# A two-layer attention step on one core: cached keys and values loaded in blocks of 128 rows

## The reference, cut to what matters

```python
s = jnp.concatenate([
    jnp.einsum('bqhcd,bkhcd->bhcqk', q, k_past), jnp.einsum('bqhcd,bkhcd->bhcqk', q, k_new)], axis=-1) * scale
p = jax.nn.softmax(s, axis=-1)
pd = p[:, :, 0] - lam * p[:, :, 1]
o = jnp.einsum('bhqk,bkhe->bqhe', pd[..., :p_len], v_past) + jnp.einsum('bhqk,bkhe->bqhe', pd[..., p_len:], v_new)
```

```python
s_past = einsum('bqhd,bkhd->bhqk', q, k_past) * scale + f_q[..., None] - f_bht[:, :, None, :p_len]
```

## Time and profile before

| what | us |
|---|---|
| median of 3 runs | 2518.02 (2517.57 to 2519.05) |
| the profiled execution, own time | 2516.69 |
| its span, first to last instruction | 2514.2 |
| stage A, about | 629 to 765 of the span |
| stage B, about | 1865 to 2015 of the span |

### The profile page before, as it was taken

The page is one execution under the profiler, slowest core; times in us unless marked ns, Lnnn a source line. Parts: engine busy times, 40 slices in busy tenths (PEclk is TensorE's granted clock), DMA queues, the critical chain, the costliest instruction groups (busy, mean ns, idle before and its releaser), DMA issues.

```text
span 2514.2 us, 46820 instructions
## 1 busy us (share of the span) xinstructions
PE 2463.0 (98%) x18869; PEld 2333.4 (93%) x18869; DVE 1687.4 (67%) x2936; ACT 1134.2 (45%) x2261; POOL 192.3 (8%) x136
## 2 busy tenths in 40 slices
PE   8999999999898999999999999999998899999998
PEld 8999999888678999999988999999986599999998
DVE  7777676322797886758625786858626677868585
ACT  6443444101785543435413553525327755535254
POOL 0000000543000000000044000000120000000000
PEclk9999999999999999999999999999999999999999
DMA  4323232233762232323233332222359631322222
GB/s 129 91 72 95 70 99 61 82 117 102 293 236 76 63 105 62 99 76 91 62 80 125 106 109 81 74 87 72 114 192 314 226 109 47 111 79 74 86 72 80
DMA packets 267136, 271.45 MB, mean 108 GB/s; under 512 B 13785, under 2 KB 224034, under 8 KB 266930
## 3 DMA queue, kind: packets, MB, share of 16 engines
q1 hardware_dynamic: 261184, 253.45, 32.4%
q10 hardware_dynamic: 5746, 15.12, 1.7%
HBM read 255.02 MB, written 13.51 MB: 107 GB/s over the span
## 4 chain that ended last, share of the span: by engine, by line
PE 90%; DVE 5%; ACT 2%; issue 2%; DMA 1%; DVEq 0%; POOL 0%; ACTq 0%
PE PS L769 40%; PE PS L875 24%; PE PS L956 10%; PE PS L719 7%; PE PS L707 2%; PE PS L1014 1%; PE PS L702 1%; PE PS L1157 1%; PE PS L1115 1%; DMA R<-in_cache_b_k_dram 1%; PE PS L1076 1%; PE PS L1087 1%; DVE x_area L2050 0%; DVE R L2005 0%; ACT R L1646 0%
## 5 line engine op out<-in xcount | busy, mean ns | idle before, releaser
L769 PE MATMUL PS<-x_area,w_area 128*128 128x320 f32 x3096 | 482.1, 309 | 0.0
L769 PEld LDWEIGHTS PS<-x_area,w_area 128*128 128x128 f32 x3096 | 461.0, 188 | 0.2 <-DVE w_area L1991 0.2
L875 PE MATMUL PS<-r_area,w_area 128*128 128x320 f32 x2568 | 393.3, 309 | 0.0
L875 PEld LDWEIGHTS PS<-r_area,w_area 128*128 128x128 f32 x2568 | 380.7, 188 | 0.8 <-DVE r_area L2183 0.8
L1435 ACT ACTIVATE w_area<-R 128x512 fp32r<-128x512 f32 x341 | 212.7, 628 | 200.4 <-PE PS L769 133.0
L1982 DVE TENSOR_TENSOR w_area<-R,w_area 128x768 fp32r<-128x768 f32 (+2 forms) x143 | 132.4, 926 | 218.5 <-ACT w_area L1420 216.9
L1991 DVE TENSOR_TENSOR w_area<-R,w_area 128x512 fp32r<-128x512 f32 x341 | 234.4, 688 | 47.6 <-ACT w_area L1435 41.8
L1420 ACT ACTIVATE w_area<-R 128x768 fp32r<-128x768 f32 (+2 forms) x143 | 117.0, 818 | 308.2 <-PE PS L875 281.2
L875 PE MATMUL PS<-v_area,w_area 128*128 128x320 f32 x1620 | 253.5, 309 | 0.0
L956 PE MATMUL PS<-w_area,xn_hi 128*128 128x512 f32 x800 | 251.0, 395 | 0.0
L875 PEld LDWEIGHTS PS<-v_area,w_area 128*128 128x128 f32 x1620 | 241.5, 188 | 0.3 <-DVE v_area L2183 0.3
(11 more groups left out here) (297 smaller groups left out, 3566.6 us busy)
## 6 DMA issues: line engine op xcount, KB each, us to landing
R<-in_w_ffn_up_dram SPq DMA_DIRECT2D x88, 512.0 KB, 3.9
R<-in_w_ffn_gate_dram SPq DMA_DIRECT2D x84, 512.0 KB, 3.9
R<-in_w_ffn_down_dram SPq DMA_DIRECT2D x96, 384.0 KB, 3.2
vreg<-in_cache_a_v_dram SPq DMA_DIRECT2D x8, 2048.0 KB, 9.0
vreg<-in_cache_b_v_dram SPq DMA_DIRECT2D x8, 2048.0 KB, 9.5
R<-in_cache_a_k_dram SPq DMA_DIRECT2D x14, 1024.0 KB, 7.2
R<-in_cache_b_k_dram SPq DMA_DIRECT2D x14, 1024.0 KB, 9.8
R<-in_w_qkv_a_dram SPq DMA_DIRECT2D x24, 512.0 KB, 3.8
```

The source lines that it names most:

```text
L769: last = pe.matmul(PS[:, bank, 0:HT], a[:, k, :], b[:, k, :], start=(start and k == 0 and a is hi and b is x_hi), stop=(k == 3 and a is lo ...
L875: last = pe.matmul(out[:, h, :], a[slot][:, w], x[:, h * HT:(h + 1) * HT], start=(k == 0 and a is w_hi and x is hi), stop=(k == n - 1 and ...
```

## The change

The loads change from 1 MB of keys and 2 MB of values to blocks of 128 rows, 512 KB each in pieces of 4 KB, for keys and values alike. `Knat` becomes four row blocks. `key_turn(b, j)` turns block j of all eight heads, as many turns and copies of the same size as `key_pair` had. Each step now waits for its own block, and block k of the next but one stream can be asked for as soon as block k has been turned. Keys use two semaphores (even and odd blocks) and values two, and before asking for block k SP waits until block k-2 of the same tensor has landed. The first keys of a stage are loaded in two halves by rows, and each of the eight `first_keys` waits for both halves.

In B the keys of stream 1 stay ahead of the values; two of their blocks now stand between the forget rows. The diff, cut to its core (PE, ACT and DVE call `key_turn` at the places where they called `key_pair`, and that is left out):

```diff
 nat = R1[:, 0:2 * TB * D].rearrange("p (w t c) -> p w t c", w=2, t=TB)
-Knat = R1[:, 0:4096].rearrange("p (s k c) -> p s k c", s=2, k=PB)
+Knat = R1[:, 0:4096].rearrange("p (k c) -> p k c", k=PB)
 kTc = R1[:, 4096:8192].rearrange("p (h k) -> p h k", h=PAIR)
...
 
-def load_keys(queue, x, b, s):
-    queue.dma_start(Knat[:, s], key_rows[x][b, :, s * 512:(s + 1) * 512].rearrange("(k p) c -> p k c", p=P)).then_inc(
+def load_first_keys(queue, x, s):
+    queue.dma_start(Knat[:, 2 * s:2 * s + 2, :], key_rows[x][0, 256 * s:256 * s + 256, :].rearrange("(k p) c -> p k c", p=P)).then_inc(
         sem(f"k_in{x}{s}"), 16)
+
+def keys_landed(b, k):
+
+    return 16 + (b - 1) * 32 + (k // 2 + 1) * 16
+
+def values_landed(x, b, k):
+
+    return ("AB".index(x) * DB + b) * 32 + (k // 2 + 1) * 16
...
 
-        def keys(b, s):
-            load_keys(sp, x, b, s)
-
-        def values(b):
-            sp.dma_start(Vc, vc[b].rearrange("(k p) c -> p k c", p=P)).then_inc(sem("v_in" + x), 16)
+        def keys(b, k):
+            at = sem(f"k_in{x}{k % 2}")
+            sp.wait_ge(at, keys_landed(b, k) - 16)
+            sp.dma_start(Knat[:, k, :], key_rows[x][b, k * P:(k + 1) * P, :]).then_inc(at, 16)
+
+        def values(b, blocks):
+            for k in blocks:
+                at = sem(f"v_in{k % 2}")
+                if k >= 2:
+                    sp.wait_ge(at, values_landed(x, b, k) - 16)
+                sp.dma_start(Vc[:, k, :], vc[b][k * P:(k + 1) * P, :]).then_inc(at, 16)
...
 
-        sp.wait_ge(sem("kt_ready" + x), 4)
-        keys(1, 0)
         if x == "A":
+            sp.wait_ge(w_used, BASE["oa"])
+            values(0, range(PB))
+            sp.wait_ge(sem("kt_readyA"), 8)
+            for k in range(PB):
+                keys(1, k)
             tile(BASE["oa"], SLOT["oa"], *cols(w_o_a[0], SLOT["oa"], 0))
-            sp.wait_ge(sem("kt_readyA"), 8)
+        else:
+            sp.wait_ge(sem("kt_readyB"), 8)
+            keys(1, 0)
             keys(1, 1)
-            sp.wait_ge(w_used, BASE["oa"])
-        else:
             sp.wait_ge(w_used, BASE["ob"] - 1)
             rows(0)
             forget(0, 0)
+            keys(1, 2)
+            keys(1, 3)
             sp.wait_ge(sem("sq_used"), 4 * KB)
             forget(0, 1)
             rows(1)
-            sp.wait_ge(sem("kt_readyB"), 8)
-            keys(1, 1)
             sp.wait_ge(w_used, BASE["ob"])
-        values(0)
+            values(0, range(PB))
         for i in range(DB - 1):
+            more = i + 2 < DB
             if f_scr is not None:
                 sp.wait_ge(sem("biased" + x), i * 2 + 2)
                 forget(i + 1, 0)
                 forget(i + 1, 1)
-            if i + 2 < DB:
-                sp.wait_ge(sem("kt_ready" + x), (i + 1) * 8 + 4)
-                keys(i + 2, 0)
-            if f_scr is not None and i + 2 < PAIR:
-                sp.wait_ge(sem("nb_ready" + x), i * 4 + 4)
-                rows(i + 2)
+            for k in range(3):
+                if more:
+                    sp.wait_ge(sem("kt_ready" + x), (i + 1) * 8 + 2 * k + 2)
+                    keys(i + 2, k)
+                if k == 1 and f_scr is not None and i + 2 < PAIR:
+                    sp.wait_ge(sem("nb_ready" + x), i * 4 + 4)
+                    rows(i + 2)
             sp.wait_ge(sem("pv_ready" + x), i * 2 + 2)
-            values(i + 1)
-            if i + 2 < DB:
+            values(i + 1, (0, 1))
+            if more:
                 sp.wait_ge(sem("kt_ready" + x), (i + 1) * 8 + 8)
-                keys(i + 2, 1)
+                keys(i + 2, 3)
+            values(i + 1, (2, 3))
 
     for c in range(4):
...
 
-        pe.wait_ge(sem(f"k_in{x}{h // 4}"), 16)
+        for s in range(2):
+            pe.wait_ge(sem(f"k_in{x}{s}"), 16)
         if h >= 2:
             pe.wait_ge(sem("first_read" + x), h - 1)
         for k in range(PB):
-            last = flip(PS[:, bank, k * P:(k + 1) * P], Knat[:, h // 4, k, (h % 4) * P:(h % 4 + 1) * P])
+            last = flip(PS[:, bank, k * P:(k + 1) * P], Knat[:, k, h * P:(h + 1) * P])
         last.then_inc(sem("kt_ready" + x), 1)
...
+        reads, first_reads = (5, 2) if x == "A" else (4, 1)
+
+        def key_turn(b, j):
 
             if b == DB:
                 return
-            if j % 2 == 0:
-                pe.wait_ge(sem(f"k_in{x}{j // 2}"), b * 16 + 16)
+            pe.wait_ge(sem(f"k_in{x}{j % 2}"), keys_landed(b, j))
             if j == 0:
                 pe.wait_ge(sem("sexp_doneA" if x == "A" else "biasedB"), b * 2)
                 if x == "B" and b >= 2:
                 if x == "A" and b >= 3:
                     pe.wait_ge(sem("columns_readA"), b - 2)
             else:
-                pe.wait_ge(sem("pairs_read" + x), (b - 1) * reads + first_pair_reads + j - 1)
-            for h in range(2):
-                at = (2 * j + h) % 4 * P
-                for k in range(PB):
-                    for r in range(2):
-                        to = (4 * h + k) * 64
-                        last = half_flip(PS[:, 3 + 4 * r, to:to + 64], Knat[:, j // 2, k, at:at + P], r)
+                pe.wait_ge(sem("keys_read" + x), (b - 1) * reads + first_reads + j - 1)
+            for h in range(PAIR):
+                for r in range(2):
+                    last = half_flip(PS[:, 3 + 4 * r, 64 * h:64 * h + 64], Knat[:, j, h * P:(h + 1) * P], r)
             last.then_inc(sem("kt_ready" + x), 2)
 
         def turn(h, t):
...
 
-            pe.wait_ge(sem("v_in" + x), b * 16 + 16)
+            for k in (2, 3):
+                pe.wait_ge(sem(f"v_in{k % 2}"), values_landed(x, b, k))
             for r in range(2):
                 pe.wait_ge(sem(f"pd_read{x}{r}"), b * 2 + 2)
             for g in range(2):
...
 
-        def key_pair(b, j):
+        def key_turn(b, j):
             if b == DB:
                 return
             act.wait_ge(sem("kt_ready" + x), b * 8 + 2 * j + 2)
             for r in range(1 if x == "A" and j == 0 else 2):
-                last = act.activation(kTc[:, 2 * j:2 * j + 2, :].rearrange("p h (k r q) -> p r (h k) q", k=PB, r=2)[:, r],
-                                      PS[:, 3 + 4 * r, :].rearrange("p (n q) -> p n q", q=64), ACT.Copy)
-            last.then_inc(sem("pairs_read" + x), 1)
+                at = j * P + 64 * r
+                last = act.activation(kTc[:, :, at:at + 64], PS[:, 3 + 4 * r, :].rearrange("p (h q) -> p h q", q=64), ACT.Copy)
+            last.then_inc(sem("keys_read" + x), 1)
 
         def stream_exps(b):
...
     all_heads("A", qh)
-    load_keys(act, "A", 0, 0)
-    load_keys(act, "A", 0, 1)
+    load_first_keys(act, "A", 0)
+    load_first_keys(act, "A", 1)
     first_keys("A", 5)
     tail_rows(5, BASE["oa"])
...
-        def first_pair_uppers(b):
+        def first_uppers(b):
 
             if b == DB:
                 return
             dve.wait_ge(sem("kt_readyA"), b * 8 + 2)
-            dve.tensor_copy(kTc[:, 0:2, :].rearrange("p h (k r q) -> p r (h k) q", k=PB, r=2)[:, 1],
-                            PS[:, 7, :].rearrange("p (n q) -> p n q", q=64)).then_inc(sem("pairs_readA"), 1)
+            dve.tensor_copy(kTc[:, :, 64:P], PS[:, 7, :].rearrange("p (h q) -> p h q", q=64)).then_inc(sem("keys_readA"), 1)
 
         def stream_peaks(b):
...
```

42 lines of the change are left out of this document (20 added, 22 removed).

## The result

The changed kernel takes **2534.31 us** (median of four runs, 2530.59 to 2537.64) against 2517.80 for the kernel before beside it: ratio 1.0066 [1.0050, 1.0082], 16.5 us slower. The prediction was 2515.8, with a range to 2522.0, so it was wrong in sign and size. All medians here are of executions in the fast state; one execution of the kernel "before, store later" (10756 us) was not in it and is left out.

What follows compares the result with a forecast made beforehand. The prediction took PE, busy 98% of the span, as the bound. It summed -9.9 (smaller loads), +7.0 (start of A) and +0.7 (clock) to -2.2 us, from 2518.02 to 2515.8, range 2509.0 to 2522.0.

Steps and rivals of the forecast that it cites:

- What bounds the kernel: Whole kernel: PE is busy 98% of the span, so only its stops and lower-clock stretches can be won back.
- 10.9: Loops of A and B: us lost to PE's stops and half clock, 4.9 in A and 6.0 in B.
- (1) smaller loads, -9.9: Loops of A and B: instruction packets wait behind less data with 512 KB loads and key waits go, -9.9 us.
- stops stay: Rival, A and B: packets late for another reason than load size, only 1.4 us of key waits won; +6.3 us, chance 0.13.
- (2) the start of A, +7.0: Start of A: key block 0 queues behind values and store, landing at 643.9; a new PE stop of +7.0 us.
- the bounds: Start of A: the new stop lies between 1.5 us (landing at 638.4) and 9.8 us (asked for at 635.4, landing at 646.7).
- The clock: Start of A: a longer stop may repeat the 0.50 clock once or twice, 0 to 2.6 us, taken as +0.7.
- (3) the start of B, 0: Start of B: key blocks 2 and 3 ahead of two forget rows delay these at most 2.5 us; taken as 0.
- (4) the steady loop's slack, 0: Steady loop: value blocks 2 and 3 wait for 0 and 1, landing in about 10 of 13.2 us; no cost.
- (5) turns, copies, waits, 0: Turns and copies keep their number and size; the few extra waits for long-set semaphores cost nothing.

Runs made afterwards that it cites:

- before, store later: Kernel before, with the store of A's new values asked for in five 512 KB pieces in rounds 1 to 5 of A's loop: ratio 1.0014.
- the old order alone: Changed kernel, with A's start put back to w_o piece, then stream 1's key blocks, then values: +19.6 us to the kernel before, ratio 1.0094.
- the kernel with both edits and the store later: Changed kernel with A's start order of before, no landing waits, and A's store in pieces in rounds 1 to 5: ratio 0.9998 to before.

## Why the prediction was wrong, point by point

- **What bounds the kernel**: right. PE is the bound, the loss is all in stops and half clock in A and B, and what could be won was real (8.8 us in the medians with an eighth of the loads, against 10.9). By stages the prediction comes to about +3 us in A and -5 in B; measured were +7.0 and +10.0.
- **(1) smaller loads, -9.9**: this is the step that failed, "an instruction packet waits behind the data that a large load has put in front of it". I had one packet that moved when a 1 MB load ended, and read the size of the load into it. I also took the packet to be asked for near 657, with that load; matched with the run with an eighth of the loads, it could have started near 659.5. Values in blocks alone gave +0.2 us. In the changed kernel the packet stops sum to 1.6 us in A, but 6.5 in B, against 3.6 and 3.2 before, and in B they are longer in all ten traces with keys in blocks of 512 KB than in the seven with keys in 1 MB loads. In B the 1.4 us of key waits went. The rival "stops stay" was the right one here, and had 0.13.
- **(2) the start of A, +7.0**: mechanism right, size off: 8.7 us (645.67 against 636.94), inside the bounds. I took key block 0 to land at 643.9; it was asked for at 636.13, 0.7 us later than in the upper bound, and took 9.5 us. The clock came as said: 0.50 from 645 to 651, and PE worked 6.2 us at that level after the stop against 3.4 before. That is 1.0 to 1.2 us of loss, an estimate from rows of the same work at either level (below), where I took 0.7. (5.24 MB at 422 GB/s are 12.4 us, not 12.5.) What I missed did not change this sum but the remedy: the layout itself moves 1 MB of keys behind the eighth turn, and together with the landing waits that leaves no gain for the old order alone.
- **(3) the start of B, 0**: right. First score product to first value product, 18.8 us before and after.
- **(4) the steady loop's slack, 0**: held in A (no value wait in the changed kernel's two traces), failed in B. "Block 1 lands after 3.9" came from weight loads with nothing ahead of them. In B key block 0, 512 KB, took 6.4 to 9.4 us behind the forget rows, and, worse, I counted landings between value blocks alone, and not that SP stands at the wait for key block 0 ahead of the values. In the round shown above that made them 4.8 us late. There were 3.9 us of value waits in the profiled execution, 0.2 to 1.5 at a time in others; without landing waits B is 4.6 us shorter on average. I had listed what is queued behind an added wait only for the start of A.
- **(5) turns, copies, waits, 0**: right for the whole (2508.6 against 2508.5 us with an eighth of the loads). In A of the changed kernel an iteration takes 15.8 us instead of 15.64, 0.8 us in five, each with a wait of 0.22 us for a copy of DVE:

```profile
680.35 0.71 PE L727 MATMUL PS<-cst,R 64*128 64x64 f32 x16 [0.22 <-DVE R L2351]
...
696.16 0.72 PE L727 MATMUL PS<-cst,R 64*128 64x64 f32 x16 [0.22 <-DVE R L2351]
```

In B the known stops of after are 3.9 us of values and 6.5 of packets, against 4.6 of packets and keys before: +5.8 of the 10.0. The clock is most of the rest. PE worked 17.5 us of B at a granted clock of 0.50, against 11.6 before. At 0.50 the 32 value products above take 1.93 us, at 1.00 they take 1.08, and 16 turns take 1.12 and 0.71; by these rows the 5.9 us more are an estimate of 2 to 3 us lost. The stretches at 0.50 that the kernel before doesn't have lie at the stops of 3.70 and 2.82 us (windows in B of the changed kernel), and what is left, 1 to 2 us, was not found:

```profile
1918.00:1920.00 2.00, 2.00 (x25) 1.10 (x26) 1.22 (x5) 1.07 (x3) 0.00 (x0) 0.56 1.07 397
1920.00:1922.00 2.00, 2.00 (x16) 0.44 (x12) 0.00 (x0) 1.19 (x5) 0.00 (x0) 0.58 0.96 383
...
1989.00:1991.00 2.00, 2.00 (x44) 2.00 (x40) 0.35 (x1) 0.00 (x0) 0.00 (x0) 0.50 1.02 278
```

## What to carry to other kernels

A wait on a queue that issues loads holds back everything written behind it: before adding a throttle, list what stands behind each wait, and take the landing time from a row with the same traffic ahead, not from an idle stretch. A buffer's layout decides when its first piece comes free; check it at the start of a stage, where one load too many meets stores. And a coincidence in one window (a packet that moves as a load ends) is a guess at a mechanism: it deserves a small chance until the one-line edit that tests it alone has run.

## What the runs showed of the hardware

- TensorE's instruction packets lie on the critical path here, 0.4 to 3.7 us at a time in the kernels before and changed. A packet starts 2.3 to 2.6 us before PE goes on: 661.5 and 663.96, and in the changed kernel 1914.8, 1932.8, 1968.3 and 1917.25, 1935.12, 1970.72. The Trainium skill, Runtime: NRT & Kernel Launch, section Instruction fetch mechanics, calls the cost of crossing a 256-instruction block mostly hidden; with an eighth of the loads that is so, with the loads whole it is not.
- The DMA engines can be busy and move little. In the kernel with both edits and the store later, the windows from 1915 to 1922 us have a DMA share of 0.72 to 1.00 and move 186 to 371 GB/s, those from 1906 to 1912 have 0.98 to 1.06 and 348 to 406. In the slow stretch forget rows, asked for from 1910.5, keys and row pieces move. Its cause was not tested.

```profile
1909.00:1910.00 1.00, 1.00 (x6) 0.29 (x5) 1.00 (x3) 0.00 (x0) 0.58 (x2) 1.00 1.00 397
...
1916.00:1917.00 1.00, 0.94 (x22) 0.73 (x21) 0.55 (x4) 1.00 (x4) 0.00 (x0) 1.00 1.00 244
```
